# A two-layer model and a third block on one NeuronCore: the matmuls on a zero tile taken out

## What is computed

```python
def even_layer(x, ...):      # first layer
    u = rms_norm(x, norm_g) @ w_in
    o_f = fox_attention(q_f, k_f, v_f, f_l + b_f)   # 8 heads of 64, causal, with a learned decay
    o_r = retention(q_r, k_r, v_r) * gn_g           # 8 heads of 64, fixed decay, group norm
    return x + (concat(o_f, o_r) * silu(z)) @ w_out

def odd_layer(x, ...):       # second layer: 16 heads in 4 groups, three branches
    u = rms_norm(x, norm_g) @ w_in
    o = gate0 * compressed + gate1 * selected + gate2 * window
    return x + (o * silu(z)) @ w_out

def second_block(x, mem, ...):
    h = rmsnorm(x)           # HGRN2 scan, top-k sparse attention, attention to a memory
    x = x + concat(o_hg, o_sa, o_mem) @ w_out
    h = rmsnorm(x)
    return x + (silu(a) * b) @ w_ffn_out            # a, b = h @ w_ffn_in
```

## Time and profile before

| | us |
|---|---|
| median of 3 runs | 1838.86 |
| lowest and highest | 1823.66, 1840.61 |
| profiled execution, span | 1881.8 |
| TensorE busy in it | 1780.5 (95%) |
| VectorE, ScalarE, GpSimd busy | 660.8, 557.3, 551.9 |
| mean granted clock | 0.884 |

### The profile page before, as it was taken

One profiled execution on the slowest core, in us unless ns is written; L12 is line 12 of the kernel. 1 busy time (PEld: TensorE's weight loads), 2 busy tenths in 40 slices (PEclk: granted clock), 3 DMA queues, 4 the chain that ended last, 5 costly groups with the idle time before them and its releaser, 6 DMA issues.

```text
span 1881.8 us, 22864 instructions
## 1 busy us (share of the span) xinstructions
PE 1780.5 (95%) x8323; PEld 1414.4 (75%) x8392; DVE 660.8 (35%) x1231; ACT 557.3 (30%) x1036; POOL 551.9 (29%) x306
## 2 busy tenths in 40 slices
PE   5999999999999996999999989999898999999998
PEld 4888856677787875778777768777677788888787
DVE  4111111443312415543565242677766222211000
ACT  5121301222321141322233241555323244444220
POOL 6543300001644261000110241354000434444442
PEclk9998965657999797965799997999977999999999
DMA  7443210000333241000000221233000223233231
GB/s 205 90 98 81 75 53 12 1 0 23 88 101 89 56 135 51 2 0 0 0 0 0 64 61 45 76 87 101 1 1 1 79 78 100 89 100 98 81 101 57
DMA packets 78461, 111.87 MB, mean 59 GB/s; under 512 B 10185, under 2 KB 43121, under 8 KB 78273
## 3 DMA queue, kind: packets, MB, share of 16 engines
q1 hardware_dynamic: 74080, 105.46, 19.7%
q0 software_dynamic: 2240, 5.60, 1.0%
q10 hardware_dynamic: 2080, 0.01, 0.1%
HBM read 108.93 MB, written 2.10 MB: 59 GB/s over the span
## 4 chain that ended last, share of the span: by engine, by line
PE 83%; DVE 7%; issue 5%; POOL 2%; ACT 1%; DMA 1%; DVEq 1%; another core or an unknown queue 0%; ACTq 0%; POOLq 0%
PE psum L1346 17%; PE psum L1347 17%; PE psum L1348 16%; PE psum L1353 7%; PE psum L1419 7%; PE psum L1409 4%; PE psum L1328 3%; PE psum L1454 2%; PE psum L1463 2%; PE psum L1340 2%; PE psum L1579 1%; POOL weight_low L397 1%; PE psum L1668 1%; DMA gains<-in_even_norm_g 1%; PE psum L1581 1%
## 5 line engine op out<-in xcount | busy, mean ns | idle before, releaser
L397 POOL TENSOR_TENSOR weight_low<-weight_raw,weight_high 128x1024 fp32r<-128x1024 f32 x188 | 452.3, 2409 | 663.8 <-ACT weight_high L544 322.9
L1346 PE MATMUL psum<-act_high,weight_high 128*128 128x512 f32 x704 | 274.3, 390 | 0.0
L1348 PE MATMUL psum<-act_high,weight_low 128*128 128x512 f32 x704 | 273.9, 389 | 0.0
L1347 PE MATMUL psum<-act_low,weight_high 128*128 128x512 f32 x704 | 273.9, 389 | 0.0
L544 ACT ACTIVATE weight_high<-weight_raw 128x1024 fp32r<-128x1024 f32 x104 | 110.2, 1060 | 397.3 <-PE psum L1348 393.6
L1346 PE MATMUL psum<-weight_high,act_high 128*128 128x512 f32 x560 | 223.2, 399 | 2.6 <-DVE odd_k L1014 2.6
L1347 PE MATMUL psum<-weight_low,act_high 128*128 128x512 f32 x560 | 220.6, 394 | 0.0
L1348 PE MATMUL psum<-weight_high,act_low 128*128 128x512 f32 x560 | 220.1, 393 | 0.0
L884 DVE TENSOR_REDUCE minus_max<-psum 128x1 f32<-128x128 f32 (+1 forms) x192 | 92.9, 484 | 196.1 <-PE psum L1581 116.9
L1348 PEld LDWEIGHTS psum<-act_high,weight_low 128*128 128x128 f32 x704 | 132.1, 188 | 27.5
L1347 PEld LDWEIGHTS psum<-act_low,weight_high 128*128 128x128 f32 x704 | 132.2, 188 | 27.4
(11 more groups left out here) (309 smaller groups left out, 2775.8 us busy)
## 6 DMA issues: line engine op xcount, KB each, us to landing
weight_raw<-in_w_ffn_in SPq DMA_DIRECT2D x88, 256.0 KB
weight_raw<-in_even_w_in SPq DMA_DIRECT2D x32, 512.0 KB
weight_raw<-in_w_in SPq DMA_DIRECT2D x24, 512.0 KB
weight_raw<-in_w_ffn_out SPq DMA_DIRECT2D x22, 512.0 KB
weight_raw<-in_odd_w_in SPq DMA_DIRECT2D x20, 512.0 KB
weight_raw<-in_even_w_out SPq DMA_DIRECT2D x8, 512.0 KB
weight_raw<-in_odd_w_in SPq DMA_DIRECT2D x16, 256.0 KB
weight_raw<-in_odd_w_out SPq DMA_DIRECT2D x8, 512.0 KB
```

The costliest lines, as they stand in the source:

```text
L397: nc.gpsimd.tensor_tensor(WL[:, r], RAW[:, r], WH[:, r].bitcast(f32), ALU.subtract).then_inc(split_ready, 1)
L1346: mm(bank, hi_l, hi_r, start=start, stop=False, skip_group_check=True)
L1347: mm(bank, hi_l, lo_r, start=False, stop=False, skip_group_check=True)
L1348: return mm(bank, lo_l, hi_r, start=False, stop=stop, skip_group_check=True)
```

## The change

The function `keep_clock`, its 21 executions (15 places in the text), the constants for its rounds, the zero tile and GpSimd's one memset of it go. Nothing else is touched: the waits behind the removed loops stay where they are.

```diff
-W_RET, W_FOX, W_GN, W_ODD, W_ODDY, W_HG, W_HGO = 5, 3, 3, 2, 4, 5, 1
-W_PAIRS, W_CMP, W_NORMS, W_RES = 1, 2, 4, 1
...
-        ZERO = sb(ctx, "zero_bf16", [P, T], bf16)
...
-            nc.gpsimd.memset(ZERO[:, :], 0.0).then_inc(sem("zero_ready"), 1)
...
-            def keep_clock(bank, rounds):
-
-                pe.wait_ge(sem("zero_ready"), 1)
-                with pe.Fori(0, rounds):
-                    for _ in range(8):
-                        mm(PS[:, bank, :], ZERO[:, 0:P], ZERO[:, :], start=True, stop=True, skip_group_check=True)
...
-            keep_clock(6, W_RET)
             wait_group(pe, "even_z")
             pe.wait_ge(sem("forget_parts"), 1)
             with pe.Fori(0, 2) as i:
-                keep_clock(6, W_PAIRS)
                 pe.wait_ge(sem("ret_k_staged"), i + 1)
...
-            keep_clock(6, W_FOX)
             pe.wait_ge(sem("ret_weighted"), CREDIT + 32)
             pe.wait_ge(sem("ret_taken"), CREDIT + 8)
             pe.wait_ge(sem("decay_rows"), 48)
             with pe.Fori(0, 2) as i:
-                keep_clock(7, W_PAIRS)
                 pe.wait_ge(sem("q_staged"), i + 1)
...
-            keep_clock(7, W_GN)
             attention_done("odd")
             features("even_y")
             project("even_out", True, "even_y")
-            keep_clock(7, W_RES)
             features("odd")
...
             for i in range(2):
-                keep_clock(3, W_CMP)
                 pe.wait_ge(sem("cmp_low"), i + 1)
...
-            keep_clock(3, W_CMP // 2)
             pe.wait_ge(sem("odd_tables"), 16 * 11)
             pe.wait_ge(sem("cmp_hidden"), 4)
...
             with pe.Fori(0, 4) as i:
-                keep_clock(7, W_ODD)
                 pe.wait_ge(sem("q_staged"), 2 + i + 1)
...
-            keep_clock(7, W_ODDY)
             attention_done("sa")
             features("odd_y")
             project("odd_out", True, "odd_y")
...
-            keep_clock(7, W_NORMS)
             features("sec")
...
-            keep_clock(7, W_RES)
             pe.wait_ge(sem("sa_normed"), 3)
...
             pe.wait_ge(sem("sa_features"), 8)
-            keep_clock(7, W_HG)
             wait_group(pe, "hg_n")
...
-            keep_clock(0, W_HGO)
             features("sec_y", normed=False)
             project("sec_out", True, "sec_y")
-            keep_clock(7, W_RES)
             features("ffn")
```

## The result

| | before | after |
|---|---|---|
| median of the runs, us | 1839.73 | 2018.76 |
| lowest, highest | 1823.66, 1939.30 | 2016.13, 2022.38 |
| span of the profiled execution | 1881.8 | 2014.4 |
| mean granted clock in it | 0.884 | 0.798 |

The ratio after to before is 1.1015 (95% interval 1.0941 to 1.1088): the kernel without the zero matmuls is 10% slower. The changed kernel repeats itself within 6.3 us; the kernel before doesn't, which the experiments come back to. Executions of it that stand out by a lower clock are left out of the ratios.

The account below looks back on a forecast made before the run. TensorE was taken to bound the kernel, at a granted clock of 1.2 or 2.4 GHz. The terms, +126.4 of them from the passes, summed to +132.4 us on 1881.8: 2014 us, range 1925 to 2045, chance 0.70.

Parts of the forecast that it names:

- The passes: Second layer's attention: three of four passes go from 57.08 to 99.20 us, 3 x 42.12 = +126.4 us.
- the step: At the four passes: the bare wait leaves the clock at 0.50, and a pass begun cold stays cold.
- the one in which the loop wakes itself: Rival at the four passes: each is cold only some 10 us; 1863 us, between 1846 and 1875; chance 0.08.
- the cold second pass: Second layer's attention, profiled before the change: 99.20 us at 0.51, taken as showing that a cold pass stays cold.
- The base: Starting time: profiled 1881.8 us with one cold pass, median 1838.86 probably with all four warm; both lead to 2014.
- The direct savings: Time by which zero matmuls outlast the waits behind them: 0.8 + 2.8 + 1.9 + 2.5 = 8 us.
- the bounds of 242.2 and 245.2: Ahead of the retention: when the decay table lands; ends -6.8 and +3.7 us, taken as 0.
- The first attention's halves: First layer's attention: both halves lose their warm starts and take about 52.0 us each, +4.1 us.
- The stretch to the end of the compressed branch: After the first layer's attention net -0.2 us, in the compressed branch net -1.0 us.
- The 32 transposes after the first attention: After the first layer's attention: start 1.9 us sooner but cold, costing 1.7 us; net -0.2.
- The scan: HGRN2 scan with the last attention: first two levels lose their warm run, +5 us; ends 0 and +20.

## Why the prediction was right

- **The passes, +126.4 forecast, +128.8 measured.** Both halves of the step held: the bare wait of 4.32 us loses the clock whenever it was up, and a pass begun cold stays cold. Two of the four passes showed 3.4 us at full clock, at their very ends, and lost it in the wait; that is why two are 99.2 and two 100.5 us, where I had 99.2 for each. Of the rivals, the one in which the loop wakes itself was wrong for these loops as they stand and right for the passes with all rows. Its price was given twice and not alike: near +10 in one place, and 17 + 6 = 23 on the median, which is 19 less than the profiled execution, in the other. What decides between holding and waking, the rows, stood nowhere in the prediction; it took the behaviour of the cold second pass over without a cause.
- **The base.** That the median run of the kernel before has all passes warm, and the profiled execution one cold, fitted (1881.8 - 42.1 = 1839.7 against a median of 1839.73), but that is luck: the median is that of four runs, and runs of this kernel lay 100 us apart.
- **The direct savings** came as worked out from the waits behind: 2.65 for 2.8 ahead of the first attention, 0.68 for 0.8 ahead of the passes, and 0.75 net for 0 up to the end of the retention, where the decay table landed at 243.7, between the bounds of 242.2 and 245.2.
- **Mis-sized terms.** The first attention's halves lost 2.3 us, not 4.1, since without zero matmuls they still caught a little of full clock at their ends (0.52). The stretch to the end of the compressed branch gained 0.9 us more than forecast; the narrow projection in it was cold for 14 us in this execution where it was 20 before, and it was anything from 14 to 20 in the other kernels, whatever their edit. The 32 transposes after the first attention, cold at first, took 6.6 us in place of 4.8, which is 1.8 us more, near the 1.7 that I had taken.
- **The scan, +5 forecast, +5.05 measured,** is right by luck: in the kernels here it took 118 to 142 us, at clocks from 0.71 to 0.92. The median moved by 179 us where the two profiled executions, with one cold pass before, moved by 132.6.

## What to carry to other kernels

A matmul that does no useful work is judged by the clock of the stage behind it, not by its own time: here 360 of them (86 us of TensorE's busy time for the 323 recorded) added some 8 us to the end, by the prediction's estimate, because they ran in waits, and their removal costs 10%. Filler that leaves a rest of the wait idle may lose the clock all the same, so it is best sized to the wait. There is a second cure: a loop that can't keep the clock may be given all 128 rows in matmuls that are there anyway, with zeros in the new rows. That took no more time on TensorE (a half of the first attention at 0.50 is 50.5 us with the rows and was 51.4 without), it lengthens the staging where zeros have to be set beside the data, and alone it was worth about as much as all the filler; the two together are the fastest, 3.6% under the kernel before. Look in the windows for two stretches of the same work at different clocks before trusting any duration.

## What the runs showed of the hardware

- TensorE busy from end to end doesn't bring the clock up: 100.48 us busy of 100.48 at 0.50. The rows of the array that the matmuls use count as well, also where they hold zeros: 128 rows in place of 6, in one of the five matmuls that make a score, is the difference, in the kernel with zero matmuls, between passes of 100 us and of 57.
- There is a gap between holding and waking. The passes hold 1.00 when they begin with it and don't wake from 0.50; with two zero matmuls per unit, or with full rows in the score matmuls, they wake. The first attention with its decay matmul filled holds 1.00 and doesn't wake; with full rows in its scores it wasn't tried. The retention with its scores filled lost the clock in the wait and woke in the middle of its first half (27.8 us at 0.73).
- 26 float32 transposes held the clock up to the next pass as zero matmuls do (57.08 us at 1.00 twice), and it also came up while they ran (at 860.5). Transposes in bfloat16 weren't tried.
- With all rows in the score matmuls a pass at 1.00 takes 52.70 us and not 57.08, at the same columns and counts. Most of it sits where rows change: behind the third score matmul of 256 columns the bias matmul, which has 128 rows, starts after 0.21 us when the score has 64 rows and after 0.12 us when it has 128. Why, the runs don't tell.
